# The prompt tile's 128 expert slots spread 44, 56 and 28 over three stages, with TensorE adding the expert value rows of the middle stage

## The reference, cut to what matters

```
h  = rmsnorm(x) * (1 + scale1) + shift1
h @ w_in -> HGRN2 q | i | f_fwd | f_bwd | gate | GQA q | k | v | merge gates A, B
mixer A: bidirectional gated linear recurrence (the "scans")
mixer B: grouped-query attention
y  = (sigmoid(gA) * (oA @ w_oa) + sigmoid(gB) * (oB @ w_ob)) @ w_out ;  x = x + gate1 * y
x  = x + gate2 * PEER(rmsnorm(x) * (1 + scale2) + shift2)
```

```
u = jnp.take(w_u, idx, axis=0)
act = gelu(einsum('nhkd,nd->nhk', u, xb))
v = jnp.take(w_v, idx, axis=0)
return einsum('nhk,nhkd->nd', (g * act), v)
```

## Time and profile before

| what | us |
|---|---|
| median of 3 runs | 2538.37 |
| lowest, highest | 2535.85, 2538.88 |
| profiled execution, its span (no other time of it is given) | 2543.3 |
| stage "win" with slots 0 to 51 | about 336 to 552 |
| stage "merged" (latent scans and attention), slots 52 to 69 | about 552 to 870 |
| stage "mix", slots 70 to 127 | about 870 to 1097 |

### The profile page before, as it was taken

One profiled execution on the slowest core, in us unless ns is written; L12 is line 12 of the kernel. 1 busy time (PEld: TensorE's weight loads), 2 busy tenths in 40 slices (PEclk: granted clock), 3 DMA queues, 4 the chain that ended last, 5 costly groups with the idle time before them and its releaser, 6 DMA issues. The chain is left out here.

```text
span 2543.3 us, 27323 instructions
## 1 busy us (share of the span) xinstructions
PE 2005.6 (79%) x6925; PEld 1104.9 (43%) x6925; DVE 1749.4 (69%) x3969; ACT 945.2 (37%) x2456; POOL 941.2 (37%) x774
## 2 busy tenths in 40 slices
PE   6978898946677798668698776877768787687876
PEld 2577846745566543267455222322223222232222
DVE  2732278886776678767787777777777777777764
ACT  1402145223343434312333444444444444344443
POOL 0020012232222222303233554656545665456654
PEclk9998999977888899879899998999999999999999
DMA  8744678851111389859798999999999999999997
GB/s 317 289 152 154 231 291 322 332 192 67 67 67 60 150 332 337 337 203 401 272 372 317 422 421 393 420 422 422 421 404 415 422 422 421 407 401 421 422 422 330
DMA packets 113299, 805.53 MB, mean 317 GB/s; under 512 B 12596, under 2 KB 14006, under 8 KB 17046
## 3 DMA queue, kind: packets, MB, share of 16 engines
q0 software_dynamic: 93760, 680.96, 66.5%
q1 hardware_dynamic: 17704, 118.17, 12.6%
q10 hardware_dynamic: 1712, 4.98, 0.5%
HBM read 800.79 MB, written 3.28 MB: 316 GB/s over the span
## 5 line engine op out<-in xcount | busy, mean ns | idle before, releaser
L1213 POOL DMA_INDIRECT RG<-in_uv,idxs x264 | 356.5, 1351 | 562.0 <-DVE pl L1440 322.1
L957 ACT ACTIVATE agel<-apre 128x1 f32<-128x1 f32 x640 | 129.3, 202 | 984.6 <-DVE apre L1412 981.2
L600 PE MATMUL pl<-RG,BP 128*128 128x512 f32 x576 | 294.9, 638 | 106.8 <-ACT BP L973 102.3
L600 PE MATMUL pl<-RING,BP 128*128 128x512 f32 x576 | 281.7, 621 | 62.1 <-ACT BP L973 59.6
L1412 DVE CUSTOM_DVE_ANT_0 R<-RG,AB 128x1024 f32<-128x1024 f32 x201 | 246.8, 1230 | 100.8 <-DMA RG<-in_uv,idxs 79.8
L1213 POOL DMA_INDIRECT RING<-in_uv,idxs x168 | 248.9, 1482 | 158.7 <-PE pl L600 69.4
L1412 DVE CUSTOM_DVE_ANT_0 R<-RING,AB 128x1024 f32<-128x1024 f32 x168 | 205.9, 1226 | 95.6 <-DMA RING<-in_uv,idxs 77.2
L625 PE MATMUL pa<-HL,RING 128*128 128x512 f32 (+2 forms) x800 | 243.7, 461 | 4.2 <-DVEq L457 2.6
L600 PEld LDWEIGHTS pl<-RG,BP 128*128 128x128 f32 x576 | 100.1, 192 | 294.5 <-ACT BP L973 214.0
L973 ACT ACTIVATE BP<-CT,wexp 128x128 f32<-128x128 f32 x480 | 192.7, 401 | 51.1 <-PE pl L600 12.9
L600 PEld LDWEIGHTS pl<-RING,BP 128*128 128x128 f32 x576 | 104.3, 194 | 234.2 <-ACT BP L973 139.7
(11 more groups left out here) (288 smaller groups left out, 3261.0 us busy)
## 6 DMA issues: line engine op xcount, KB each, us to landing
RING<-in_in_slabs SPq DMA_DIRECT2D x42, 1024.0 KB, 6.0
RING<-in_pq_slabs SPq DMA_DIRECT2D x24, 1152.0 KB, 5.5
RING<-in_ada_slabs SPq DMA_DIRECT2D x16, 1024.0 KB, 5.0
RING<-in_out_slabs SPq DMA_DIRECT2D x12, 1024.0 KB, 9.1
RG<-in_col_slabs POOLq DMA_DIRECT2D x8, 1024.0 KB, 6.9
RING<-in_o_slabs SPq DMA_DIRECT2D x8, 1024.0 KB
RG<-in_uv,idxs POOLq DMA_INDIRECT x297
RING<-in_uv,idxs POOLq DMA_INDIRECT x168
```

The costliest lines, as they stand in the source:

```text
L600: last = nc.tensor.matmul(acc[:, c * 512:(c + 1) * 512], DG[:, k % 2, :], bufs[k % len(bufs)][:, D + c * 512:D + (c + 1) * 512], start=Fal ...
L957: A(agel[:, par, k:k + 1], apre[:, par, k:k + 1], ACT.Gelu).then_inc(gel_done, 1)
L1213: nc.gpsimd.indirect_dma_start(out=bufs[b], out_offset=None, in_=uv, in_offset=bass.IndirectOffsetOnAxis(ap=idxs[:, par, k:k + 1], axis=0) ...
```

## The change

The prompt's slots are spread 44, 56 and 28 over the three stages (50, 20 and 58 before). In "merged" a pair of slots has its place at the forward group of each of the 28 latent levels, instead of being spread by shares. For these 56 slots (numbers 44 to 99, `ROWS_LO` to `ROWS_HI`) DVE no longer adds the V row: ACT makes the diagonal, and PE adds it to PL (`v_prompt`), at a place of its own, `ROWS_AT`: after everything of that level's beat, before the next level's first group. POOL's lead is 2 slots there. PL is zeroed by PE (`edge(PL, True, pl_ready)`) in place of a DVE memset.

```
-STAGES = (("win", 50, ...), ("merged", 20, ...), ("mix", 58, ...),
+NWIN, NMERGED, NMIX = 44, 56, 28
+ROWS_LO, ROWS_HI = NWIN, NWIN + NMERGED
...
+    levels_at = [names.index(("lvl", u, l, 0)) for u in range(1, NT) for l in range(LEVELS)]
+        if stage == "merged":
+            for k in range(count):
+                i = k // 2 * 2 * len(levels_at) // count
+                rows_at[len(slot_at)] = levels_at[i + 1] - 1 if i + 1 < len(levels_at) else hi - 1
+                slot_at.append(levels_at[i])
...
+            def v_prompt(n):
+                pe.wait_ge(dg_done, n - ROWS_LO + 1)
+                if n == ROWS_LO:
+                    pe.wait_ge(v_done, n + V0)
+                for c in range(2):
+                    last = nc.tensor.matmul(PL[:, c * 512:(c + 1) * 512], DG[:, n % 2, :],
+                                            GA[n % NGA][:, D + c * 512:D + (c + 1) * 512], start=False,
+                                            stop=False, skip_group_check=True)
+                last.then_inc(v_done, 1)
+            rows = Beside(v_prompt, lambda n: 0, ROWS_AT)
...
                     for d in range(2):
+                        rows.before(("lvl", u, l, d))
                         pe.wait_ge(hg_ready[d], (LEVELS + 1) * u + l + 1)
...
-                    if isinstance(n, int) and n < NSLOT:
+                    if isinstance(n, int) and n < TSLOT:
+                        i = n
+                        act.wait_ge(v_done, n - 1 + V0)
...
-                            -POOL_LEAD)
+                            lambda n: -2 if ROWS_LO + 2 <= n < ROWS_HI + NGA else -POOL_LEAD)
...
-                if (t == 0 and n) or (t and k % 2):
+                if (t == 0 and n and not ROWS_LO < n <= ROWS_HI) or (t and k % 2):
                     v_row(n - 1)
...
-            step(V.memset(PL[:, :], 0.0))
+            dve.wait_ge(pl_ready, 1)
```

More of the change, by code:

```diff
@@ L80 @@
 EXPO_AT = 5
[L82 to L85, removed]
+NWIN, NMERGED, NMIX = 44, 56, 28
+ROWS_LO, ROWS_HI = NWIN, NWIN + NMERGED
+STAGES = (("win", NWIN, {"winT": 6.0, "win": 3.0}),
+          ("merged", NMERGED, {}),
+          ("mix", NMIX, {"oT": 1.0, "gate_a": 6.9, "gate_b": 6.9, "ra": 3.5, "rb": 3.5}),
           ("post1", 0, {"y": 3.5, "x2T": 2.0, "h2": 2.0, "qp": 2.0, "ss": 1.0}),
@@ L236, in settle @@
         return at
-    slot_at = []
-    for (_, count, share), lo, hi in zip(STAGES, marks, marks[1:]):
+    slot_at, rows_at = [], {}
+    levels_at = [names.index(("lvl", u, l, 0)) for u in range(1, NT) for l in range(LEVELS)]
+    for (stage, count, share), lo, hi in zip(STAGES, marks, marks[1:]):
+        if stage == "merged":
[3 more added lines that the diff above has]
+                slot_at.append(levels_at[i])
+            continue
         reach = np.cumsum([share[names[i][0]] for i in range(lo, hi)])
@@ L247, in plan_groups @@
     assert len(slot_at) == NSLOT
-    return names, place, slot_at
-NAMES, PLACE, SLOT_AT = plan_groups()
+    return names, place, slot_at, rows_at
+NAMES, PLACE, SLOT_AT, ROWS_AT = plan_groups()
 INDEX = {name: i for i, name in enumerate(NAMES)}
@@ L459, in build, with __init__ @@
         class Beside:
-            def __init__(self, slot, shift):
-                self.slot, self.shift, self.next, self.first, self.end = slot, shift, 0, 0, 0
+            def __init__(self, slot, shift, at=SLOT_AT):
+                self.slot, self.shift, self.at, self.next, self.first, self.end = slot, shift, at, 0, 0, 0
             def place(self, n):
-                n += self.shift
-                return SLOT_AT[max(n, self.first)] if n < self.end else len(NAMES)
+                n += self.shift(n)
+                return self.at[max(n, self.first)] if n < self.end else len(NAMES)
             def before(self, name):
@@ L475, in open, with span @@
             def open(self, t):
-                self.first, self.end = t * TSLOT, min((t + 1) * TSLOT, NSLOT)
+                self.span(t * TSLOT, min((t + 1) * TSLOT, NSLOT))
+            def span(self, first, end):
+                self.first, self.end = first, end
             def rest(self):
@@ L607, in start @@
                 beside.before(name)
+                rows.before(name)
                 for b, turn in zip(*PLACE[name][:2]):
@@ L906, in _ @@
             post(0)
+            pe.wait_ge(zb_ready, 1)
+            edge(PL, True, pl_ready)
             pe.wait_ge(hT_ready, NT)
@@ L910, in _ @@
             pe.wait_ge(win_ready[W_I], 2 * NT)
+            rows.span(ROWS_LO, ROWS_HI)
             turn_qk([1, 2, 3, 4])
@@ L915, in _ @@
                 tail(NT - 1, i)
+            rows.rest()
             mix(1)
-            pe.wait_ge(zb_ready, 1)
             for b in (4, 5):
```

16 lines of the change are left out of this document (9 added, 7 removed).

## The result

The kernel after takes 2632.7 us (median of 5 runs, 2626.7 to 2638.1), the kernel before on the same chip 2535.9 us (5 runs, 2531.5 to 2538.9). The ratio is 1.0373, with a 95% interval of 1.0355 to 1.0392: 3.7% slower. The forecast was 2638 us.

A forecast was written before the change was run, and what follows sets the result against it. Gathers bound the later part; "win" and "mix" were DVE's, "merged" a chain of latencies. -28 - 44 + 172 = +100 us on 2543.3 gives 2643, less 5 for the median: 2638 us, range 2575 to 2690.

The forecast's parts named there:

- The step that decides: Scan levels: V rows on PE follow the transposes and values, delaying the next level's matmuls, for which DVE waits, 3.94 us.
- "win", -28: Before the first latent level: eight slots fewer on DVE, with PE as cover; -28 us, bounds -20 and -32.
- "mix", -44: Merge stage: thirty slots fewer on DVE leave PE the bound at 183 us; -44 us, bounds -27 and -50.
- The bound "PE without a wait": Merge stage: the far bound of the gain, -50 us, if PE never waits.
- V rows in the scans, +110: "merged": V rows on PE delay each of 28 levels by 3.94 us, 110 us in all.
- DVE's part of 56 slots, +123 on top of 257: "merged": 2.2 us of DVE per slot lies on the path, 123 us, added to 257 us of bare scans and attention.
- the slower burst cancel against the tail piece: Pair level: 2.5 us of PE's slower burst and previous unit's tail on DVE; one recurs, one vanishes, taken to cancel.
- The hidden rivals: Scans: V rows' 110 us lie beside DVE's work, wholly (2528 us, 11%) or half (2583 us, 14%).
- Cold in every level: Scans: PE work at 1.2 GHz adds 5.7 us a level, 2798 us (2%); a third of it 2690; 7% together.
- Gathers late: Scans: waits for gathers before dots, 0.38 us each, add 21 us for 56 dots, 2659 us; 3%.
- Behind the stages, 0: After the mix stage: gathers are the limit and the change does not touch them; no difference.

The follow-up runs named there:

- e1: Kernel after without the 56 V rows on PE beside the scans, one 128-column zero matmul in place of each: 2555.8 us.
- e2: Kernel after with PE adding a pair's V rows one beat later, ahead of that beat's transposes: 2575.4 us.
- e9: Kernel after with 90 zero matmuls of 128 columns in each beat of the scans, ahead of the transposes: 2656.8 us.
- e11: Kernel after with slots 44, 40, 44, V rows one beat later, 41 padding instructions at DVE's start and a rewritten POOL loop: 2541.5 us.
- e3: Kernel after with the 56 V rows back on DVE, slots' places kept: 2605.3 us.
- e12: Kernel after with slots 44, 40, 44, V rows one beat later and 80 short DVE instructions in the second mix stage: 2538.8 us.

## Why the prediction was right, and where its terms were off

The step that decides held: the V rows stand in the half of a level in which DVE waits for PE, so they lengthen the chain. The kernel came out slower by 3.7% where 3.9% was forecast. That the time agrees so well is in part luck, as the terms show.

- **"win", -28: measured -28.5.** PE was the cover, as forecast: its waits for ACT fell from 38.6 us (the 24.2 of the earlier trace rows and 14.4 of two other kinds) to 16.8, and its busy time by 8.1 us at a granted clock of 0.96 in place of 0.90. The longest wait is 14.6 us, still for ACT. Equal programs differ by some 9 us in this start, so the half microsecond is chance.
- **"mix", -44: measured -53.8, beyond the bound of -50.** The mechanism held: DVE is busy 85 of 169 us, the forecast was 87, and PE's wait of 27.4 us at the end is 0.9 now. The term assumed PE's busy time of the earlier trace rows. But that was at a granted clock of 0.89, and a PE that no longer waits ran at 1.00: the same matmuls took 167.3 us instead of 177. The bound "PE without a wait" was no bound, since the busy time itself depended on the waits. In full: the stage was forecast at 183 us and took 167.7, 9.7 less busy time and 5.6 less waiting; the forecast subtracted it from a window of 227 us, 5.5 us wider than the stage by its marks (221.5), which took some of the error away.
- **V rows in the scans, +110: measured +75 by e1.** This is the mis-sized term. They stand where the forecast had them, each in a run between values and the next level's matmuls, with DVE waiting behind. e1's 75 us is what they cost net of the colder clock without them and of the diagonals still waited for. The term also took ACT's diagonals to be on time; they were late six times, 6.2 us in all. e2 shows that the sum depended on the place: a beat later they cost 15.
- **DVE's part of 56 slots, +123 on top of 257: measured 149** (406.1 - 257). Its 26 us of excess and the V rows' 35 us of shortfall offset each other in part, which is why 490 met 481. The excess is about what e1's DVE waits at the head of its updates have over before's, 47.6 against 18 us. The clock belongs here: the forecast let the slower burst cancel against the tail piece, and e9 shows some 22 us of half clock in the levels of after. That the two are the same time is likely, not shown.
- **The hidden rivals** (2528 and 2583): the first is refuted for this place, since the V rows cost 75 us by e1 and DVE's waits of 127 us at L1602 are what the text named as the sign. The second is refuted by the time, but not so clearly as a term: its 55 us for the V rows lie 20 us from the 75, the forecast's 110 lie 35 us from it. It was DVE's part that kept the time away from 2583. The Trainium skill, "Perfetto Trace Analysis", section "Optimization Strategy", says that interleaving regimes with different most-contended engines may improve performance. Here that came out true for the transfers alone. No engine was the bound in the scans, and work put between two waits of the chain added to it; with e2's place the kernel was still 1.6% slower than before.
- **Cold in every level**: true in kind, not in size. Fifteen levels gained 0.1 to 2.7 us in e9. Their granted clock in after was 0.69 to 0.87, and each has a wait of PE of 2.8 to 6.5 us. The Trainium skill, "TensorE: Matmul & The Clock Gate", section "HAM oscillation — how this bites in real kernels", says that bursts of matmuls shorter than the waits between them start at the low clock again and again. These levels agree.
- **Gathers late**: not seen. DMA's share is 0.36, and no wait of DVE for a gather is listed in the stretch.
- **Behind the stages, 0: measured +7.8.** The prediction held that nothing there changes. The loops' code doesn't, but the number of DVE instructions ahead of it does, and tile 4 has two idles of 5.3 us.

The sum was 20 us too high at the end of the stages, and the 8 us behind them brought it to within 12 us of after's span. The forecast took 4.9 us off for before's long profiled execution, and after's time lies 1.8 us over its span: that leaves 5 us between 2638 and 2632.7. The agreement is better than the terms were.

## What to carry to other kernels

Free DMA share in a stage says that transfers fit there, not that their consumers do: in a chain in which two engines wait for each other in turn, new work makes the chain longer unless it stands in its own engine's wait. Read from the timeline on which side of that wait the new work goes; here the same 56 V rows cost 75 us behind it and 15 in it. And ask what the later place holds up: in e2 buffers came free a beat later, and with them the gathers and what stands behind them on their engine. Last, look at the order of an engine's instructions in the new trace before a test is read: e11's edit left it as it was. A busy time taken as a bound must be taken at the clock that will be granted once the waits are gone.

## What the hardware showed that was not expected

- A loop on DVE can cost 4.6 to 5.5 us at a jump back, with nothing in its own code changed: 11 of the 14 profiled kernels had it (not before, e3 and e12), in a tile that depended on the number of instructions ahead, and it came with about ten more packets on the instruction queue for each tile. Two such jumps a tile are 8 to 11 us, as much as many edits that are tried on this kernel would bring.
- What PE's clock gives is worth reading stage by stage. The mix stage took 177 us of PE at a granted clock of 0.89 and 167 at 1.00 for the same work.
- Filling waits of about 5 us with 2.4 us of zeros did not hold the clock (0.88 over 522 to 900 us); 5.2 us of zeros did (0.96, and 1.00 in 21 of 28 levels). Where a beat had little or no wait the zeros made the level longer, by up to 4.4 us with 90 of them.
- Two executions of the same code differ in single levels of the scans by up to 1.6 us, and there the granted clock differs with them (0.77 and 14.9 us, 0.69 and 16.6 us).
